# Two transformer blocks on one core: the mixers' input projections taken from the unscaled residual, with the norm's factor applied afterwards

## The reference

```python
for l in range(DEPTH):                                   # 2 layers
    h = rmsnorm(x, attn_norm_w[l])
    proj = h @ w_in[l]
    (z, xbc, dt_raw, sc_b, sc_c, sc_h, q, k_c, v_c, k_s, v_s, k_w, v_w, g_nsa) = split(proj)
    y_ssd = ssd_mixer(z, xbc, dt_raw, ...)               # conv, scan over 8 heads, gated rmsnorm
    y_sc  = sc_b * causal_dwconv(sc_c * sc_h, sc_conv_w[l])
    y_nsa = nsa_mixer(q, k_c, v_c, k_s, v_s, k_w, v_w, g_nsa, ...)
    x = x + concatenate([y_ssd, y_sc, y_nsa]) @ w_out[l]
    h = rmsnorm(x, ffn_norm_w[l])
    u = causal_dwconv(h @ ffn_w_up[l], ...)
    x = x + (silu(gate) * val) @ ffn_w_down[l]
```

## Time and profile before

| | us |
|---|---|
| median of three timed runs | 2304.95 (2304.45 to 2306.74) |
| the profiled execution | 2303.9 |
| its span in the trace | 2302.1 |
| PE busy | 2272.1 |
| DVE busy | 1691.4 |
| ACT busy | 946.7 |

### The profile page before, as it was taken

One profiled execution on the slowest core, in us unless ns is written; L12 is line 12 of the kernel. 1 busy time (PEld: TensorE's weight loads), 2 busy tenths in 40 slices (PEclk: granted clock), 3 DMA queues, 4 the chain that ended last, 5 costly groups with the idle time before them and its releaser, 6 DMA issues.

```text
span 2302.1 us, 35308 instructions
## 1 busy us (share of the span) xinstructions
PE 2272.1 (99%) x14436; PEld 2017.2 (88%) x14436; DVE 1691.4 (73%) x2780; ACT 946.7 (41%) x1413; POOL 112.7 (5%) x77
## 2 busy tenths in 40 slices
PE   9999999999999999999999999999999999999998
PEld 9799999799998888888779888888888888989997
DVE  6889878889889848845455883884885673797775
ACT  5766645766552122235553221222321222475343
POOL 0010010010010000010001000001000001001001
PEclk9999999999999999999999999999999999999999
DMA  7345476255546545532121553553354452414543
GB/s 268 141 157 188 155 245 220 101 202 184 180 151 207 191 142 192 182 124 83 51 74 56 183 184 127 173 184 127 140 195 160 135 177 100 147 38 140 181 158 127
DMA packets 66881, 355.08 MB, mean 154 GB/s; under 512 B 7328, under 2 KB 10528, under 8 KB 42912
## 3 DMA queue, kind: packets, MB, share of 16 engines
q1 hardware_dynamic: 65888, 352.23, 44.6%
q10 hardware_dynamic: 832, 0.59, 0.1%
HBM read 351.75 MB, written 1.05 MB: 153 GB/s over the span
## 4 chain that ended last, share of the span: by engine, by line
PE 91%; DVE 6%; ACT 2%; DMA 1%; issue 1%; SPq 0%; DVEq 0%; ACTq 0%
PE bank L526 89%; DVE sb_w_lo L2186 2%; ACT sb_w_hi L1430 1%; DVE sb_products L2220 1%; DMA sb_raw<-w_l_in 1%; PE bank L1382 1%; PE bank L1256 0%; ACT sb_mid L1430 0%; DVE sb_mid L2768 0%; DVE sb_latP L3001 0%; DVE sb_nP L2871 0%; DVE sb_decays L2883 0%; PE bank L1059 0%; ACT sb_decays L1430 0%; DVE sb_mid L2940 0%
## 5 line engine op out<-in xcount | busy, mean ns | idle before, releaser
L2186 DVE TENSOR_TENSOR sb_w_lo<-sb_raw,sb_w_hi 128x2048 fp32r<-128x2048 f32 (+3 forms) x280 | 564.0, 2014 | 125.5 <-ACT sb_w_hi L1430 122.4
L1430 ACT ACTIVATE sb_w_hi<-sb_raw 128x2048 fp32r<-128x2048 f32 (+5 forms) x301 | 491.5, 1634 | 384.3 <-PE bank L526 382.7
L526 PE MATMUL bank<-sb_f_pair,sb_w_hi 128*128 128x256 f32 (+1 forms) x2090 | 523.0, 339 | 5.2 <-DVE sb_w_lo L2186 4.2
L526 PE MATMUL bank<-sb_h_hi,sb_w_hi 128*128 128x512 f32 (+1 forms) x1400 | 510.8, 365 | 0.6 <-DVE sb_w_lo L2186 0.4
L526 PE MATMUL bank<-sb_h_lo,sb_w_hi 128*128 128x512 f32 (+1 forms) x1400 | 507.3, 362 | 0.0
L526 PE MATMUL bank<-sb_h_hi,sb_w_lo 128*128 128x512 f32 (+1 forms) x1400 | 507.3, 362 | 0.0
L526 PEld LDWEIGHTS bank<-sb_f_pair,sb_w_hi 128*128 128x128 f32 x2090 | 360.2, 190 | 50.9 <-DVE sb_w_lo L2186 7.2
L2220 DVE CUSTOM_DVE_ANT_0 sb_products<-sb_raw,sb_cond,sb_params 128x1024 f32<-128x1024 f32 x282 | 362.5, 1285 | 32.2 <-DVEq L2222 15.8
L526 PE MATMUL bank<-sb_f_pair,sb_w_lo 128*128 128x256 f32 (+1 forms) x1122 | 365.9, 326 | 0.0
L526 PEld LDWEIGHTS bank<-sb_h_hi,sb_w_hi 128*128 128x128 f32 x1400 | 264.2, 189 | 42.8 <-issue 0.9
L526 PEld LDWEIGHTS bank<-sb_h_lo,sb_w_hi 128*128 128x128 f32 x1400 | 264.2, 189 | 41.4 <-issue 0.5
(11 more groups left out here) (316 smaller groups left out, 2912.3 us busy)
## 6 DMA issues: line engine op xcount, KB each, us to landing
sb_raw<-w_mod SPq DMA_DIRECT2D x144, 512.0 KB, 3.3
sb_raw<-w_l_up SPq DMA_DIRECT2D x44, 1024.0 KB, 4.8
sb_raw<-w_l_in SPq DMA_DIRECT2D x22, 1024.0 KB, 6.4
sb_raw<-w_l_down SPq DMA_DIRECT2D x32, 704.0 KB, 5.1
sb_raw<-w_m0a_up SPq DMA_DIRECT2D x22, 1024.0 KB, 4.9
sb_raw<-w_m0b_up SPq DMA_DIRECT2D x22, 1024.0 KB, 4.8
sb_raw<-w_m1a_up SPq DMA_DIRECT2D x22, 1024.0 KB, 4.8
sb_raw<-w_m1b_up SPq DMA_DIRECT2D x22, 1024.0 KB, 4.8
```

What stands on the lines that cost most here:

```text
L526: return nc.tensor.matmul(out, lhsT, rhs, start=start, stop=stop, skip_group_check=True)
L1430: return nc.scalar.activation(out, in_, func, **kw)
L2186: V.tensor_tensor(split_part(*at, w_lo[s]), landed_part(*at, raw[raw_slot(*at)]), split_part(*at, w_hi[s]).bitcast(F32), ALU.subtract).the ...
```

## The change

Projections are made from residual times gain, without the token's factor. So panel 0 can start before the sums of squares are known. PE makes the sums behind panel 0 (`first_sums`, `token_sums`) and spreads the factor inside panel 1. The factor is then applied where results are taken out:

- panels 3 to 9 and 11 leave their banks through DVE (new `scale_in(j)`), no longer through ACT; for panels 3 to 8 ACT's `evacuate(j)` reads what DVE has written. Panel 9 takes the squared factor, since it is multiplied with panel 10.
- keys and queries take the factor with the rotary tables (`turns`), `kvv` with its copies, panel 0 with ACT's copies.
- on ACT `ahead(j)` now stands ahead of `evacuate(j)` for most panels.
- in layer 1 ACT and DVE split each tile of the residual while the last projection of layer 0 is still running; one chunk of the modulation is computed earlier in the layer (`IN_ORDER[1]` in place of `IN_ORDER[5]`).
- the transfers of parameters and constants are issued behind more panels, the gain's transfer first, and the first panel comes in two pieces.
- the inner norm takes its root and reciprocal by token, and PE spreads it (`head_rstd`).

```diff
-for ... ("l1_in", (IN_ORDER[0], IN_ORDER[5], IN_ORDER[7]))
+for ... ("l1_in", (IN_ORDER[0], IN_ORDER[1], IN_ORDER[7]))
...
-                if (name, n) == ("l0_in", 1):
+                if (name, n) == ("l0_in", IN_ORDER[3]):
                     sp.dma_start(params[:, KD:PARAM_W], params_d[:, KD:PARAM_W]).then_inc(S("params_in"), 16)
-                if (name, n) == ("l0_in", IN_ORDER[2]):
+                if (name, n) == ("l0_in", IN_ORDER[4]):
                     sp.dma_start(consts[:, P:CONST_W], consts_d[:, P:CONST_W]).then_inc(S("consts_in"), 16)
...
+            def token_sums():
+
+                b = take("norm_sq", KD)
+                a = take("sq_added", KD - 2)
+                c = take("rms_done", 1)
+                pe.wait_ge(S("rms_done"), c)
+                pe.wait_ge(S("sq_added"), a + KD - 2)
+                pe.wait_ge(S("norm_sq"), b + KD)
+                sum_tokens(sq_sum, True, False)
+                sum_tokens(sq[:, 1, :], False, True).then_inc(S("norm_sum"), 1)
...
+                def taken(i):
+
+                    if 3 <= i < 10 or i == 11:
+                        pe.wait_ge(S("in_scaled"), q + (i - 2 if i < 10 else 8))
+                    else:
+                        pe.wait_ge(S("in_evac"), e + min(i, 9) + 1)
...
                 def evacuate(j):
                     n = IN_ORDER[j]
-                    panel_done(L + "_in", n)
                     src = in_bank(j)[:, :].rearrange("p (a t) -> p a t", a=2)
+                    u = U[:, 2 * n - 2:2 * n, PAD:UW]
+                    if 3 <= j < 9:
+                        act.wait_ge(S("in_scaled"), q + j - 2)
+                    else:
+                        panel_done(L + "_in", n)
...
                 for j in range(6):
-                    evacuate(j)
-                    ahead(j)
+                    if j in (1, 2):
+                        evacuate(j)
+                        ahead(j)
+                    else:
+                        ahead(j)
+                        evacuate(j)
...
+                def scale_in(j):
+
+                    n = IN_ORDER[j]
+                    panel_done(f"l{l}_in", n)
+                    x = (rstd_squared if j == 9 else rstd_of).unsqueeze(1).to_broadcast([P, 2, T])
+                    V.tensor_tensor(U[:, 2 * n - 2:2 * n, PAD:UW], in_bank(j)[:, :].rearrange("p (a t) -> p a t", a=2), x,
+                                    ALU.mult).then_inc(S("in_scaled"), 1)
...
                 dt_soft()
+                if l:
+                    mod_part("l1_in", IN_ORDER[1], 0)
+                    mod_part("l1_in", IN_ORDER[1], 1)
                 in_low(4)
                 keys()
+                scale_in(3)
                 in_low(5)
                 queries()
                 conv(0)
+                scale_in(4)
                 in_low(6)
...
+                if l == 0:
+                    conditions(0, 4)
+                scale_in(5)
                 in_low(7)
                 if l == 0:
-                    conditions(0, 8)
+                    conditions(4, 8)
                 conv(4)
                 conv(5)
+                scale_in(6)
...
-                in_mod(5)
                 if l == 0:
                     conditions(8, 12)
+                scale_in(7)
                 in_low(8)
                 conv(6)
                 conv(7)
                 if l == 0:
                     conditions(12, 16)
+                scale_in(8)
...
                 mats(3)
+                scale_in(9)
                 out(2)
                 maxes(1)
                 out(3)
                 maxes(2)
+                probs(1)
                 in_low(11)
-                probs(1)
                 probs(2)
                 maxes(3)
                 short_conv(0)
                 short_conv(1)
                 probs(3)
+                scale_in(11)
                 low(f"l{l}_out", 0)
```

More of the change, by code:

```diff
@@ L867, in mixers @@
                 h = h_thin
[L869 to L874, removed]
-                if l == 0:
[L876 to L894, removed]
-                else:
[L896 to L901, removed]
@@ L902, in mixers @@
-                last.then_inc(S("panels_used"), 1)
+                e = take("in_evac", 10)
+                q = take("in_scaled", 8)
+                front_high, front_low = w_hi[half_slot(L + "_in", 0)], w_lo[half_slot(L + "_in", 0)]
+                if l:
+                    pe.wait_ge(S("high"), SPLIT_AT[L + "_in", 0] + 1)
+                for k in range(KD):
+                    if l == 0 and k < KD - 2:
+                        pe.wait_ge(S("front_high"), k // 2 + 1)
+                    elif l == 0:
+                        pe.wait_ge(S("high"), 1)
+                    ready(k)
+                    for tb in range(2):
+                        o, x = bank[2 + tb][:, 0:T], both(h, slice(None), k, slice(tb * P, (tb + 1) * P))
+                        mm(o, x[0], front_high[:, k * TM:k * TM + T], k == 0, False)
+                        mm(o, x[1], front_high[:, k * TM:k * TM + T], False, False)
@@ new lines, in mixers @@
+                for k in range(KD):
+                    if l == 0 and k == 0:
+                        pe.wait_ge(S("front_low"), 1)
+                    if k == (0 if l else KD // 2):
+                        panel(L + "_in", 0)
+                    for tb in range(2):
+                        last = mm(bank[2 + tb][:, 0:T], h[0][:, k, tb * P:(tb + 1) * P],
+                                  front_low[:, k * TM:k * TM + T], False, k == KD - 1)
+                last.then_inc(S("panels_used"), 1)
@@ L1942, in nsa_high, with root_y @@
                     run(h_thin[0][:, 6 + i, :], nsa_y[:, i, :], ACT.Copy).then_inc(S("mix_high"), 1)
-                square_y, root_y = square_apart(4, lambda k: yss[:, k, :], T, 1)
+                square_y, _ = square_apart(4, lambda k: yss[:, k, :], T, 1)
+                head_sums = take("norm_sum", 0)
+                def root_y():
+                    act.wait_ge(S("norm_sum"), head_sums)
+                    sums = bank[1][:, 0:8].rearrange("p (b c) -> p b c", b=2)[:, :, 0]
+                    run(rstd[:, 0:2], sums, ACT.Sqrt, bias=eps[:, :]).then_inc(S("rms_done"), 1)
                 def squares(*ks):
@@ L2418, in body @@
                     ahead()
+                    if after == "l1_in" and n % per == per - 1 and n >= per:
+                        second_input(m - 1)
                 sweep(name, KD * per, body, after, defer=last)
```

232 lines of the change are left out of this document (124 added, 108 removed).

## The result

The changed kernel took 2325.38 us (median of 4 runs, 2324.67 to 2327.40), the kernel before 2304.98 beside it: ratio 1.0089, 95% interval 1.0076 to 1.0102. The prediction said 2312, at most 2317. The direction was right, the size was off by a factor of three.

What follows compares the result with a forecast made beforehand. PE, busy 2272.1 of 2302.1 us, bounds the kernel; the change loads DVE, which has least room. Layer 0 +2.2 and layer 1 +4.9 make +7.1 on 2303.9, 2311.0, by the median 2312; range 2303 to 2317.

Steps and rivals of the forecast that it cites:

- the array slows after a stop: Rival, chance 0.10: stops of 4.2 and 6.0 us send PE to half clock, 2.2 us more, twice: 2316.4.
- the wait for `cond_diag`: Middle of layer 0: PE's wait of 0.9 us goes, counted as -0.2.
- the small steps: Layer 0: if they hide half behind each other, its total is +2.2 us instead of +3.0; +2.2 was taken.
- The start of layer 0: Panel 0 begins at about 8.1 us instead of 12.47, sums of squares behind it: -3.4 us.
- Layer 1's start: Panel 0 follows layer 0's last products at 338.4: -4.7, less sums 0.95 and spread 0.55, gives -3.2 us.
- DVE's queue: Forecast, chance 0.53: DVE's 30.8 us in the middle make PE wait 4.2 (layer 0), 6.0 (layer 1); panel 8 3.0.
- The tail: Behind panel 8: panels 9 and 10 +1.2 (layer 0), +2.5 (layer 1); flips -1.6 and -2.1; layer 0's end -0.2.
- the two hand-overs: End of layer 0: the inner norm's extra hand-overs round PE, within -0.2 us for the whole end.
- DVE doesn't hold PE: Rival, chance 0.12: DVE's middle work is 27.8 us or less, `hid_parts` is never waited for: -9.8, 2295.
- The same waits, but smaller behind panel 8: Rival, chance 0.25: 3.7 us charged behind panel 8 in both layers lie mostly under PE's other products: +3, 2308.

Runs made afterwards that it cites:

- start_sums: Changed kernel plus 12 useless products ahead of the first panel and two between each pair of layer 0's sums of squares: 2327.46 us, ratio 1.0095 to the kernel before.
- filled: Changed kernel plus useless TensorE products at the start and, in each layer, before the hidden layer's product, panel 8 and the inner norm's spread: 2317.47 us, ratio 1.0044.
- low8_first: Changed kernel with panel 8's low part put back ahead of scale_in(7) on DVE, both layers: 2317.49 us, ratio 1.0042 to the kernel before.
- best_nofill: Changed kernel, orders mended (hidden copy and gelu, panel 8's low part, modulation chunk, scale_in(9)), no useless products added: 2308.47 us, ratio 1.0006 to the kernel before.

## Why the prediction was wrong, point by point

**The step that failed is the last rival, "the array slows after a stop".** The forecast's own sum had the clock at nothing; the rival had the right mechanism with a chance of 0.10, priced at 2.2 us for each of two stops. Measured: six stretches with 1.7 or 3.4 us of missing clock each, 15.5 in all, which cost some 11 us: 9.2 for the five from 59 us on, and 1.5 for the first, by which panel 1 with the spread was slower than in `start_sums`. The size of one stretch was near; what was wrong is where it was counted. Only the stops of 4 us and more were to be followed by it, when the stop of 2.98 at panel 8 of layer 0 was too, and the waits of 1.49 at 132 us and 1.40 at 426 us, and the sums of four columns at the start.

The cited rule of the Trainium skill (TensorE: Matmul & The Clock Gate, "HAM oscillation — how this bites in real kernels") agrees with these runs in the main: half clock was paid for again behind the stops, six times in one execution, though not behind each of them. By it the rival should have been part of the forecast, not a tenth of it.

**The rest of the sum was short too.** Without the clock's 11 us the changed kernel would stand some 10 us behind the one before, at about 2315 by the median (an estimate): inside the forecast's own range, and 3 us above its 7.1. By layer it is 3.9 us for layer 0, forecast 2.2, and 6.2 for layer 1, forecast 4.9. In the prediction's account of layer 0 two steps do not add up: the wait for `cond_diag` is read as 0.9 and taken off as 0.2, and 0.8, -0.2 and 3.0 are 3.6, not the +2.8 at which it puts PE behind panel 8; the total of +3.0 is added up rightly from the terms. Halving the small steps to +2.2 was a guess.

**The start of layer 0** gave 0.5 instead of 3.4 us. The first product stood at 9.68, not 8.1: ACT had the last two squares of the residual ahead of its copy of the weights, and these waited for x. That is 1.6 us. The transfers of x on ACT's queue now stand behind the gain's, are issued 0.45 later (1.19 against 0.74), and take 5.8 us to land where they took 4.6; what makes them slower is not shown. The sums took 2.2 (forecast 2.35), and panel 1 with the spread took 7.8 instead of 6.3: the first stretch at half clock. **Layer 1's start** was right: panel 0 stands directly behind the last product of layer 0, 4.8 us sooner than before, and with the sums and the spread behind it -3.6 are left at panel 2, against -3.2.

**DVE's queue** was right in the places named for the middle. From the low part of panel 3 to the end of `scale_in(5)` 30.5 us (forecast 30.8), the wait for `hid_parts` 4.38 (4.2), at panel 8 2.98 in both layers (3.0). In layer 1 0.47, 1.33 and 3.54, 5.3 together (6.0). `scale_in` took 0.69 (0.684).

**The tail** was near: the wait for `nP` at the flips of unit 1 is gone; in layer 0 panel 9 waited 0.22 and panel 10 not at all, in layer 1 they waited 1.40 and 0.86. Not seen was the 1.49 us in each layer for DVE's reciprocal by token, which stands behind the low part of the first output panel: the two hand-overs that I had put at -0.2 with the rest.

**The other rivals.** "DVE doesn't hold PE" is refuted by the 30.5 us. "The same waits, but smaller behind panel 8" holds for layer 0, where panels 9 and 10 waited 0.2 against 1.2 in the sum, but not for layer 1 (1.40 and 0.86 against 2.5), and the whole came out above the forecast's sum, not below it.

**What stays open.** Which activity exactly makes the clock fall: it fell behind most stops of 2.4 us and more, at varying delay, behind the four-column sums in `filled`, in nine of eleven kernels behind the wait of 1.40 for panel 9, in four of eleven behind the one of 1.44 for `decays`, and not behind the waits of 1.57 us for `nP` in the kernel before. How much of the difference between 0.9995 and 0.9989 is the move of `scale_in(9)` and how much the clock's own scatter.

## What to carry to other kernels

When one engine is nearly always busy, a wait of 3 us that you add to it can cost more than 3 us, since here its clock often fell behind one: look at the granted clock of the stretch behind each stop, and price the two together. Do not take the missing clock for the price: compare the same two events in a run that keeps the clock. An edit that gives an engine work early and takes the slack from its supplier gives nothing until the supplier's queue is re-ordered; here moving four calls and adding some products of no use took the ratio from 1.0089 to 0.9989, and of the 6.6 us that the earlier starts had promised 2.4 were left. When a wait is taken away, look for the next instruction behind the same blocked one: by the ratios the copy alone gained 4 us, the copy with the gelu 10.

## What the runs showed of the hardware

The half clock does not come at a fixed distance behind a stop. With the same start the granted clock fell at 18 us in the changed kernel and between 9 and 12 in five others, and a stop of 2.98 us at 412 was followed by 12 us at 1.00 before it fell at 427, behind a further wait of 1.40; without the first stop (low8_first) it fell behind that wait all the same. The eleven runs of one program (best_nofill) differ by 8 us in this way, and their mean granted clock goes with their time. In the kernel before, whose 21 runs beside best_nofill lie between 2304.2 and 2311.0 us at 0.996 to 0.999, it does so only weakly (correlation -0.50), so its own scatter has another cause too, which stays open.
